# A head's turns of the second layer on two buffers and spread over steps, its output norm and turn apart, the last projection in three parts

## The reference, cut to what matters

```python
q, k, v, g = jnp.split(h @ w_in, 4, axis=-1)          # h: 512 tokens, or the 256 of the context
q, k = rms_norm(q), rms_norm(k)                       # over 64; then rope on the 512 tokens
s = jnp.einsum('bqhcd,bkhcd->bchqk', q, k) * HEAD_DIM ** -0.5   # k: all 768 tokens
p = jax.nn.softmax(s, axis=-1)
a = p[:, 0] - lam * p[:, 1]
o = jnp.einsum('bhqk,bkhv->bqhv', a, v)
o = rms_norm(o, head_norm) * (1.0 - lambda_init)      # over the 128 of a head
out_x = (o * jax.nn.silu(g)) @ w_out                  # 1024 x 1024
x = x + gate * out_x
```

## Time and profile before

| | us |
|---|---|
| median of 3 runs (lowest, highest) | 1281.92 (1280.1, 1285.08) |
| the profiled execution's own time | 1278.96 |
| its span, first to last instruction | 1277.1 |
| PE busy (share of the span) | 1182.1 (93%) |
| DVE, ACT, POOL busy | 618.0, 340.5, 213.8 |
| mean granted TensorE clock | 0.985 |
| layer 1's loop, first scores to last product | 864.2 to 1236.9 |

### The profile page before, as it was taken

How to read it: one execution, slowest core, us unless ns; L and a number is a source line. 1 busy time by engine, 2 the same in 40 slices (tenths; PEclk the granted TensorE clock), 3 DMA queues, 4 the chain that set the end, 5 groups by cost and what they waited for, 6 DMA issues and landing times.

```text
span 1277.1 us, 12416 instructions
## 1 busy us (share of the span) xinstructions
PE 1182.1 (93%) x4543; PEld 635.0 (50%) x4543; DVE 618.0 (48%) x1218; ACT 340.5 (27%) x746; POOL 213.8 (17%) x198
## 2 busy tenths in 40 slices
PE   3699999999999999999999999999999998878878
PEld 0455667565555444555544444444455444445543
DVE  0466662367786646666601235403454633435553
ACT  1411113112222234544400121103233323324430
POOL 2200000657662310000000004200121300000000
PEclk9899999999999999999999999999999999899999
DMA  9701102014434111001003041201011100100001
GB/s 312 269 1 37 66 27 105 1 64 160 174 132 171 52 50 50 1 1 50 1 1 115 1 144 46 86 0 66 26 42 66 66 34 16 51 1 1 1 1 66
DMA packets 40466, 81.50 MB, mean 64 GB/s; under 512 B 2470, under 2 KB 3975, under 8 KB 40407
## 3 DMA queue, kind: packets, MB, share of 16 engines
q1 hardware_dynamic: 36165, 68.83, 15.3%
q10 hardware_dynamic: 3122, 8.57, 1.9%
q0 software_dynamic: 1120, 3.32, 1.0%
HBM read 78.58 MB, written 2.13 MB: 63 GB/s over the span
## 4 chain that ended last, share of the span: by engine, by line
PE 87%; DVE 4%; ACT 3%; DMA 3%; issue 2%; POOL 1%; SPq 1%; DVEq 0%; ACTq 0%
PE ps L656 43%; PE ps L905 9%; PE ps L833 6%; PE ps L941 4%; PE ps L786 3%; PE ps L815 3%; PE ps L963 3%; PE ps L802 2%; PE ps L953 2%; PE ps L852 2%; PE ps L695 2%; PE ps L884 2%; PE ps L874 2%; DMA ring<-in_mod_w_dram 1%; ACT xs_all L1618 1%
## 5 line engine op out<-in xcount | busy, mean ns | idle before, releaser
L656 PE MATMUL ps<-ring,hT 128*128 128x512 f32 (+1 forms) x832 | 348.9, 577 | 1.0 <-DVE hT L1078 1.0
L656 PEld LDWEIGHTS ps<-ring,hT 128*128 128x128 f32 x832 | 158.0, 193 | 173.6 <-issue 167.4
L656 PE MATMUL ps<-hT,ring 128*128 128x256 f32 (+1 forms) x512 | 169.2, 487 | 3.5 <-DVE pool_mem L1094 2.0
L1663 POOL TENSOR_SCALAR stat<-stat 128x8 f32<-128x8 f32 (+3 forms) x52 | 22.8, 438 | 761.9 <-DVE stat L1240 258.0
L656 PEld LDWEIGHTS ps<-hT,ring 128*128 128x128 f32 x512 | 96.1, 190 | 73.2 <-issue 65.8
L1272 DVE TENSOR_REDUCE stat<-ps 128x1 f32<-128x768 f32 x64 | 60.9, 952 | 65.1 <-PE ps L941 65.1
L833 PE MATMUL ps<-ring,hT 128*128 128x512 f32 x192 | 88.9, 594 | 0.8 <-DVE pool_mem L1295 0.8
L905 PE MATMUL ps<-ring,hT 128*128 128x512 f32 x192 | 85.7, 593 | 1.8 <-DMA ring<-in_ev_w_out_dram 1.8
L1337 DVE TENSOR_TENSOR pool_mem<-ps,pool_mem 128x512 f32<-128x512 f32 x28 | 19.3, 690 | 112.9 <-PE ps L905 87.2
L1664 POOL TENSOR_TENSOR stat<-stat 128x8 f32<-128x8 f32 (+3 forms) x52 | 67.4, 1296 | 4.3
L1719 POOL TENSOR_TENSOR pool_mem<-consts,dtv 128x512 f32<-128x512 f32 x48 | 57.2, 1199 | 37.0 <-PE ps L786 37.0
(11 more groups left out here) (180 smaller groups left out, 1431.5 us busy)
## 6 DMA issues: line engine op xcount, KB each, us to landing
ring<-in_mod_w_dram SPq DMA_DIRECT2D x11, 2048.0 KB, 9.0
ring<-in_od_w_in_dram SPq DMA_DIRECT2D x8, 2048.0 KB, 7.8
ring<-in_ev_w_in_dram SPq DMA_DIRECT2D x7, 2048.0 KB, 8.2
ring<-in_ev_w_out_dram SPq DMA_DIRECT2D x4, 1536.0 KB, 6.6
ring<-in_od_w_out_dram SPq DMA_DIRECT2D x2, 2048.0 KB, 7.8
ring<-in_mod_w_dram ACTq DMA_DIRECT2D x1, 2048.0 KB, 15.1
xs_all<-in_x_dram POOLq DMA_DIRECT2D x4, 512.0 KB, 9.1
xs_all<-in_x_dram ACTq DMA_DIRECT2D x4, 512.0 KB, 5.6
```

The lines of the kernel that those rows point to most:

```text
L656: mm = pe.matmul(bank[:, 0:width], lhs_of(k), rhs_of(k), start=(k == 0), stop=(k == count - 1))
```

## The change

In `stages_layer1()`:

- One of the three turns of head h+1 stands in each of the steps t = 0, 1, 2 of head h, directly behind `sc1` (and so ahead of `ptr1` and `exp1`), in place of all three in step t = 3 behind `exp1`. `qT1` and `kT1` become two buffers each, by the head's parity, and ScalarE's copies wait for the scores of head h-2 (of the buffer's last user), not of h-1.
- `hnorm` of head h stands at the end of step 4h+5 (before: in step 12 or later, right behind the `pv1` that completes the head, or later), and `otr` of heads 0 to 6 at the start of steps 11, 13, 15, 19, 23, 27 and 31, ahead of `ptr1`. Head 7's stay behind the loop, with two projection units between norm and turn.
- The output projection has three parts: `out1a` over heads 0 to 3 in steps 20 to 27, `out1b` over heads 4 and 5 (steps 28 to 31 with one, one, one and two units, one more ahead of the last `pv1`, and two behind the last `hnorm`), `out1` over heads 6 and 7 at the end. Each step now has a fill unit.
- `gates` (the load of the layer's gate rows) moves from step 11 to step 10.

To find room: `decay`, `cdec` and `dtv` of layer 0 become one buffer `dcd`, whose first 768 columns are the second `kT1`; the second `qT1` is the place of the triangle masks in `consts`; the square's unused output, which went to one of these masks, has its own `o_junk`. The diff, cut to its core (the key copies change as `hq` does; unit lists, semaphores and VectorE's output stage take the new kind in).

```diff
+    fill += [("g1", 1, t) for t in range(NX)] + [("out1a", n, t) for n in range(2) for t in range(NX)]
+    fill += [("out1b", n, t) for n in range(2) for t in range(NX)]
     work = [(h, t) for h in range(C_HEADS) for t in range(NX)]
+    out_turn = {11: 0, 13: 1, 15: 2, 19: 3, 23: 4, 27: 5, 31: 6}
+    ropes = []
     st += [("hk", 0, 1), ("hq", 0), ("hk", 0, 0)]
-    for n in range(len(work) + 1):
-        if n < len(work):
-            st += [("sc1",) + work[n] + (c,) for c in range(2)]
+    for n in range(len(work)):
+        h, t = work[n]
+        st += [("sc1", h, t, c) for c in range(2)]
+        if h < C_HEADS - 1 and t < 3:
+            st.append((("hk", h + 1, 1), ("hq", h + 1), ("hk", h + 1, 0))[t])
+        if n in out_turn:
+            st.append(("otr", out_turn[n]))
         if n >= 1:
             st.append(("ptr1",) + work[n - 1])
-        if n < len(work):
-            h, t = work[n]
-            st.append(("exp1", h, t))
-            if t == NX - 1 and h < C_HEADS - 1:
-                st += [("hk", h + 1, 1), ("hq", h + 1), ("hk", h + 1, 0)]
-                if h + 1 == 3:
-                    st.append(("gates", 1))
-            st += ropes
-            ropes = []
-            st.append(("comb1", h, t))
-        now = []
-        if n < 16:
-            now = [fill.pop(0) for _ in range(1 + (n in (1, 2, 3, 9)))]
-        elif n < 20:
-            now = [gate_fill.pop(0)]
-        elif early_out and n % 3 != 2:
-            now = [early_out.pop(0)] if len(early_out) > 2 else []
+        st.append(("exp1", h, t))
+        if n == 10:
+            st.append(("gates", 1))
+        st += ropes + [("comb1", h, t)]
+        now = [fill.pop(0) for _ in range(1 + (n in (1, 2, 3, 9, 31)))]
         st += now
-        ropes += [("rope",) + u for u in now if u[0] in ("k1", "q1")]
+        ropes = [("rope",) + u for u in now if u[0] in ("k1", "q1")]
         if n >= 1:
             st.append(("pv1",) + work[n - 1])
-            if work[n - 1][1] == NX - 1:
-                late += [("hnorm", work[n - 1][0]), ("otr", work[n - 1][0])]
         if n == 16:
             st.append(("gatesum", 1))
-        if n >= 12 and n < len(work):
-            for _ in range(2):
-                if late:
-                    st.append(late.pop(0))
-    st += late[:1] + early_out + late[1:]
+        if n >= 5 and n % 4 == 1:
+            st.append(("hnorm", n // 4 - 1))
+    st += [("ptr1",) + work[-1], fill.pop(0), ("pv1",) + work[-1], ("hnorm", C_HEADS - 1)] + fill
+    st.append(("otr", C_HEADS - 1))
     st += [("out1", n, t) for n in range(2) for t in range(NX)]
...
-    if kind == "out1a":
+    if kind in ("out1a", "out1b"):
         return [("out1", stage[1])]
...
-        qT1 = carve(L1, SEQ)
-        kT1 = carve(L1 + 1024, TOK)
+        qT1 = [carve(L1, SEQ), consts[:, P:5 * P]]
+        kT1 = [carve(L1 + 1024, TOK), dcd[:, 0:TOK]]
...
-                    first = 0 if kind == "out1a" else C_HEADS // 2
+                    first, count = {"out1a": (0, 4), "out1b": (4, 2), "out1": (6, 2)}[kind]
...
                     if kind == "hq":
-                        if h >= 1:
-                            act.wait_ge(sc_ready, SC1[("sc1", h - 1, NX - 1, 1)] + 1)
-                        A.copy(qT1, bank).then_inc(done_sem(stage), 1)
+                        if h >= 2:
+                            act.wait_ge(sc_ready, SC1[("sc1", h - 2, NX - 1, 1)] + 1)
+                        A.copy(qT1[h % 2], bank).then_inc(done_sem(stage), 1)
...
-                    A.activation(le, bank_of(stage)[:, 0:P], ACT.Square, scale=rinv[:, r:r + 1],
+                    A.activation(o_junk, bank_of(stage)[:, 0:P], ACT.Square, scale=rinv[:, r:r + 1],
```

More of the change, by code:

```diff
@@ L178, in stages_layer1 @@
     fill += [("q1", 1, t) for t in range(NX)] + [("v1", 1, t) for t in range(NT)]
-    gate_fill = [("g1", 1, t) for t in range(NX)]
-    early_out = [("out1a", n, t) for n in range(2) for t in range(NX)]
+    fill += [("g1", 1, t) for t in range(NX)] + [("out1a", n, t) for n in range(2) for t in range(NX)]
+    fill += [("out1b", n, t) for n in range(2) for t in range(NX)]
     work = [(h, t) for h in range(C_HEADS) for t in range(NX)]
-    late, ropes = [], []
+    out_turn = {11: 0, 13: 1, 15: 2, 19: 3, 23: 4, 27: 5, 31: 6}
@@ L244 @@
 UNIT_STAGES = ("params", "mod", "modsum", "modcol", "xbc", "kvdt", "dt", "q", "ga", "z", "ytr", "out0",
-               "k1", "v1", "q1", "g1", "hq", "hk", "pv1", "otr", "out1a", "out1")
+               "k1", "v1", "q1", "g1", "hq", "hk", "pv1", "otr", "out1a", "out1b", "out1")
 UNITS = [s for s in STAGES if s[0] in UNIT_STAGES]
@@ L385, in build @@
         nsink, lam = bc[:, 344:352], bc[:, 352:356]
-        dtv = sb("dtv", 2 * 192)
+        dcd = sb("dcd", 960)
+        decay, cdec, dtv = dcd[:, 0:384], dcd[:, 384:576], dcd[:, 576:960]
         dt_v, dta_v = dtv[:, 0:192], dtv[:, 192:384]
-        decay = sb("decay", 384)
-        cdec = sb("cdec", 192)
+        o_junk = sb("o_junk", C_V)
         stat = sb("stat", 192)
@@ L479, in build @@
         lam_e = stat[:, 180:184]
-        lam_p = dtv[:, 0:256]
+        lam_p = dcd[:, 704:960]
         head_gain = stat[:, 184:185]
@@ L940, in _ @@
                             half = slice(comp * HD, (comp + 1) * HD)
-                            mm = pe.matmul(pair(n + comp)[:, lo:hi], qT1[half, t * P:(t + 1) * P], kT1[half, lo:hi],
+                            mm = pe.matmul(pair(n + comp)[:, lo:hi], qT1[h % 2][half, t * P:(t + 1) * P], kT1[h % 2][half, lo:hi],
                                            start=True, stop=True)
@@ L968, in _ @@
                     turn(stage, [g1v[:, t, a[0] * P:(a[0] + 1) * P] for t in range(NX)])
-                elif kind in ("out1a", "out1"):
-                    first = 0 if kind == "out1a" else C_HEADS // 2
+                elif kind in ("out1a", "out1b", "out1"):
+                    first, count = {"out1a": (0, 4), "out1b": (4, 2), "out1": (6, 2)}[kind]
                     if a == (0, 0):
-                        for h in range(first, first + C_HEADS // 2):
+                        for h in range(first, first + count):
                             wait_done(pe, ("otr", h))
@@ L976, in _ @@
                     project(stage, SLAB, lambda k: oT[first + k][:, a[1] * P:(a[1] + 1) * P],
-                            lambda k: w[:, first + k, :], C_HEADS // 2)
+                            lambda k: w[:, first + k, :], count)
         @block.vector
@@ L1332, in _ @@
                         tmp, gate = res_tmp1[:, u % 2, :], gate_bc1[:, n * SLAB:(n + 1) * SLAB]
+                    if stage == ("out1b", 0, 0):
+                        dve.wait_ge(early_ready, 2 * NX)
                     if stage == ("out1", 0, 0):
-                        dve.wait_ge(early_ready, 2 * NX)
+                        dve.wait_ge(middle_ready, 2 * NX)
                     if u >= 2:
@@ L1595, in _ @@
                     if kind == "hq":
-                        if h >= 1:
-                            act.wait_ge(sc_ready, SC1[("sc1", h - 1, NX - 1, 1)] + 1)
-                        A.copy(qT1, bank).then_inc(done_sem(stage), 1)
+                        if h >= 2:
+                            act.wait_ge(sc_ready, SC1[("sc1", h - 2, NX - 1, 1)] + 1)
+                        A.copy(qT1[h % 2], bank).then_inc(done_sem(stage), 1)
                     else:
                         lo, hi = ((0, SEQ), (SEQ, TOK))[a[1]]
-                        if h >= 1:
-                            act.wait_ge(sc_ready, SC1[("sc1", h - 1, NX - 1, 1)] + 1)
-                        A.copy(kT1[:, lo:hi], bank[:, 0:hi - lo]).then_inc(done_sem(stage), 1)
+                        if h >= 2:
+                            act.wait_ge(sc_ready, SC1[("sc1", h - 2, NX - 1, 1)] + 1)
+                        A.copy(kT1[h % 2][:, lo:hi], bank[:, 0:hi - lo]).then_inc(done_sem(stage), 1)
                 elif kind == "v1":
```

6 lines of the change are left out of this document (3 added, 3 removed).

## The result

| | before | after |
|---|---|---|
| median (lowest, highest), us | 1281.92 (1280.1, 1285.08) | 1224.54 (1223.62, 1224.74) |
| profiled execution, its span | 1278.96, 1277.1 | 1224.74, 1222.9 |
| mean granted clock | 0.985 | 0.994 |

The ratio is 0.9547, interval 0.9516 to 0.9578.

The account below looks back on a forecast made before the run. TensorE was taken to bound the kernel. Span 1277.1 - 42.4 - 1.1 + 6 - 12.9 + 1.7 = 1228.4, plus 1.9 around it and about half of the median's 3.0 excess: 1232 us, range 1225 to 1243.

Parts of the forecast that it names:

- the waits at the turns: Layer 1's seven waits at key turns (16.6 us) and seven for the norm before output turns (16.9 us) go.
- ScalarE's copies ahead of the exponentials: Key and query copies moved ahead of the exponentials cost 0; without cover, 0.6 us in 21 steps, 12.6.
- The two-rotation step: In the loop's first half, VectorE's two rotations made the combination 1.2 us late; this wait goes too.
- The last steps: Steps 28 to 31 and just behind the loop: VectorE's lag brings new waits, taken as 6 us, bounds 0 to 9.
- The tail: Final projection units after the last turn stay bound by TensorE; closer stores cost 0, up to 2 us late.
- The clock: Layer 1's half-clock stretches go with the waits, gaining 12.9 us; one new stretch allowed, +1.7 (bounds 0 and 5).
- the step that priced a wait as its idle time alone: Sum over layer 1 and behind its loop: removed waits counted as 42.4 and 1.1 us idle.
- the first (clock): Half-clock stretches in layer 1 are set by something other than the waits and stay: 1243 us; chance 8%.
- the second (ScalarE): Copies ahead of the exponentials are not covered, so the stall moves to ScalarE, 12.6 us: 1245; chance 8%.
- the fifth (a busy bank at the key turns): Turns still meet a busy bank as units are renumbered, half of 16.6 and their clock back: about 1245; chance 3%.
- The third: Slower than before: turns beside transposes drop the clock each step; two stretches in each give 1341 us; chance 3%.
- The fourth: VectorE keeps up in the last steps and no half-clock stretch is left: 1224 us; chance 8%.

Follow-up runs that it names:

- e1: Kernel before with only the key and query turns spread, one in each of steps t = 0, 1, 2, and two buffers: 1257.1 us, ratio 0.9796.
- e2: Kernel before with only a head's norm and its turn of outputs set two or more steps apart: 1256.02 us, ratio 0.979.
- e4: Changed kernel with a head's three turns together again in step t = 3, two buffers kept: 1252.46 us, ratio 0.9754.
- e5: Changed kernel with a head's norm and turn of outputs in one step again: 1250.05 us, ratio 0.9755.
- e6: Changed kernel with the output projection in two parts of four heads, as before: 1232.89 us, ratio 0.9617.
- e3: Kernel before with only the output projection in three parts (4, 2 and 2 heads): 1275.05 us, ratio 0.9938.
- e12: e11 with head 6's turned output also taken out by ScalarE: 1219.84 us, ratio 0.9518.
- e10: Changed kernel run once more, word for word, on another chip: 1224.11 us, ratio 0.9554.
- e11: Changed kernel with the middle unit's output stage ahead of the combination in steps 28 to 31: 1220.62 us, ratio 0.9524.
- e7: Changed kernel with the residual addition of the eight middle projection units on GpSimd in place of VectorE: 1226.14 us, ratio 0.9568.
- e8: e7 with head 6's turned output also taken out by ScalarE in place of VectorE: 1225.73 us, ratio 0.9565.

## Where the forecast was right, and which step of it failed

- **What bounds, and the waits at the turns: right.** The 16.6 and 16.9 us went in full. e1, e2, e4 and e5 each show one of them go or come back alone.
- **ScalarE's copies ahead of the exponentials cost nothing: right.** No scores wait for the exponentials in steps 1 to 29.
- **The two-rotation step:** its wait of 1.2 is 0.15 (L1354 in the waits above).
- **The last steps: right in six of seven places,** nearly to size; the last turn's 0.5 did not come. Idle time is 4.7 in all, where 6 was taken.
- **The tail: right at 0.** From TensorE's last matmul to the end of the span it is 3.9 us, and was 3.8.
- **The clock: right that it comes back.** All seven stretches went, 27.3 us with 25.8 of them busy, so half of that, 12.9, is what they had cost. The allowance of 1.7 for a new one was not needed, in two traces. Its reason was misread: the scores were to be late by 0.6 and 1.5, and the shortest wait that had brought a stretch before was 1.77. That waits bring the stretches is shown by where they stand: in the traces of before and e1 to e6 all 33 begin between 0.9 us ahead of the end of a wait of 1.57 to 3.71 us and 2.0 behind it, and where the waits went they went.
- **What failed: the step that priced a wait as its idle time alone** ("Gain 16.6", "Gain: the whole 16.9", and a sum that takes off 42.4 and 1.1 and nothing for starting again). From first scores to last matmul the kernel before took 409.0 us; less 43.5 idle and 12.9 for half clock, 352.6 of work at full speed. After it is 353.27 - 4.74 = 348.5, for the same matmuls. These 4.1 us stand in no idle column. They go with the number of waits that the profile lists in this stretch: 26 waits and 352.6 before, 22 and 352.2 in e2, 21 and 351.0 in e1, 18 and 351.1 in e3, 16 and 350.9 in e4, 14 and 350.1 in e6, 11 and 349.3 in e5, 7 and 348.5 after, 3 and 348.1 in e12. A straight line through all fourteen traces rises by 0.20 us for each wait (the line leaves out how long the waits are). What these 0.2 us are made of stays open. e1's and e4's expectations had this term before those runs; the prediction did not. Rows of the kernel before show it at one wait: the step with a turn behind it is 1044.14 - 1031.45 = 12.69 long, less 10.50 and the 1.53 of wait 0.66, where the same turn in a running stream costs 0.44.

```profile
1031.45 1.56 PE L941 MATMUL ps<-pool_mem 64*128 64x512 f32 x8
...
1043.56 0.66 PE L673 MATMUL ps<-consts,pool_mem 128*128 128x128 f32 x4 [1.53 <-DVE pool_mem L1379]
1044.14 1.56 PE L941 MATMUL ps<-pool_mem 64*128 64x512 f32 x8
```

- **The sum** gave 364.1 for the stretch from the first scores to the span's end (1228.4 - 864.3), and it took 357.2. Of the 7 us too much, 4.1 are this work, 1.7 the stretch allowed for, and 1.3 the new waits. Against it, the part ahead of layer 1's scores ran 1.4 longer with the same code: its trace has 13.7 us at half clock there, that of before 10.2, which is one stretch more. That was chance (e10, the same kernel, has 10.2 there and its first scores at 864.62), and without it the miss would have been larger.
- **The median:** 1.5 us were added since before's median lay 3.0 above its profiled execution. After lies 0.2 under. That scatter is the clock's (below), and the changed kernel has little of it. The range went down to 1225 only, though its own allowances (6, 1.7 and this 1.5) could all be unneeded together, which gives 1223 even without the 4.1 that the sum left out.
- **Two slips without weight:** the kernel before has six late steps without a unit (20, 23, 26, 29, 30, 31), not five, and 6.48 with a norm of 0.69 is 7.17, not 7.14.
- **Rivals:** the first (clock), the second (ScalarE) and the fifth (a busy bank at the key turns) did not come. The third would have needed stretches in almost every step, and there was none, though turns and transposes stand side by side: the granted clock is 1.00 from 865.70 to 1218.97. So the rule of the Trainium skill ("TensorE: Matmul & The Clock Gate", Part 4) that a transpose doesn't count as activity found no cost here. The fourth came by half, as the clock kept full while VectorE did not keep up.

## What to carry to other kernels

A wait of the engine that bounds costs more than its idle time: here layer 1 got 55.7 us shorter for 38.7 of idle time, the rest being half-clock stretches (12.9) and about 0.2 us for each wait that went (4.1). Where an engine in order waits in the middle of a step, put work there that is ready (e11: 3.5 us for one moved entry in a list), and look at each queue on which a moved operation then stands in front of something (e7). Where the many small waits of a kernel bring half-clock stretches in some executions and not in others, its runs scatter; an estimate against one profiled run must say in which part of that scatter it lies.

## What was not expected of the hardware

- The scatter of the kernel before is TensorE's clock. Beside e1 its runs went from a span of 1277.7 at a mean granted clock of 0.985 to 1286.0 at 0.979. With two levels of clock, time at half clock is twice (1 - clock) of the span: 38.3 and 54.0; half of the 15.7 between them is 7.9 of the 8.3 us. After has 0.994 to 0.996 and spreads by 1.3 (e10).
- Which wait brings a half-clock stretch is not set by its length alone: before, of seven key-turn waits of 2.37 us four had one; a wait of 3.27 before and one of 3.53 in e5 had none, while in e2 and e4 two of four of 1.57 to 1.58 had one. The same wait of 3.1 ahead of the scores of step 31 had one in e8 and none in e7. What decides stays open.
- An addition of 128x512 takes GpSimd 1.27 us against VectorE's 0.69; VectorE's operations beside it in e7 kept their length (row maxima 0.95, output stage 0.68 to 0.69; both read a PSUM bank).
